# Convolution products of an attention step: one run behind the score pair instead of single products between transposes and value products

## What is computed

```
proj = h @ w_in[layer]
q, kc, vc, ksl, vsl, kwn, vwn, gts, cb, cc, ch = jnp.split(proj, split_at, axis=-1)
...
o_attn = nsa_attention(q, kc, vc, ksl, vsl, kwn, vwn, gts, rel_bias)   # compressed, selected, window branch
o_conv = short_conv(cb, cc, ch, conv_w[layer])                         # cb * conv3(cc * ch)
mixed = jnp.concatenate([rms_norm(o_attn, ...), rms_norm(o_conv, ...)], axis=-1)
x = x + mixed @ w_out[layer]
```

## Time and profile before

| | us |
|---|---|
| median of 3 executions | 2334.39 |
| lowest, highest | 2327.37, 2335.43 |
| the profiled execution | 2332.5, with a span of 2330.7 from first to last instruction |
| TensorE busy over the span | 2216.8 (95%) |
| VectorE, ScalarE, GpSimd busy | 397.0, 277.4, 70.3 |

### The profile page before, as it was taken

The page is one execution under the profiler, slowest core; times in us unless marked ns, Lnnn a source line. Parts: engine busy times, 40 slices in busy tenths (PEclk is TensorE's granted clock), DMA queues, the critical chain, the costliest instruction groups (busy, mean ns, idle before and its releaser), DMA issues.

```text
span 2330.7 us, 29764 instructions
## 1 busy us (share of the span) xinstructions
PE 2216.8 (95%) x12796; PEld 1665.9 (71%) x12796; DVE 397.0 (17%) x1080; ACT 277.4 (12%) x752; POOL 70.3 (3%) x79
## 2 busy tenths in 40 slices
PE   7999998999999989999966999999999999999994
PEld 3556644444444445566556999999999999999994
DVE  2235422000000022254231001010000101010102
ACT  1133311000000012233100000000000000000000
POOL 1100000000000011000000000000000000000001
PEclk9999998999999989999967999999999999999997
DMA  8101106222210402000018556767777777878743
GB/s 322 56 37 37 37 9 266 77 72 72 83 62 0 200 9 72 37 37 1 1 50 356 218 221 244 282 257 287 272 281 276 277 290 283 308 289 304 289 181 118
DMA packets 43987, 382.83 MB, mean 164 GB/s; under 512 B 5362, under 2 KB 5394, under 8 KB 14544
## 3 DMA queue, kind: packets, MB, share of 16 engines
q1 hardware_dynamic: 36208, 355.68, 41.0%
q0 software_dynamic: 4768, 14.92, 2.0%
q10 hardware_dynamic: 2880, 10.32, 1.1%
HBM read 368.46 MB, written 14.54 MB: 164 GB/s over the span
## 4 chain that ended last, share of the span: by engine, by line
PE 93%; DVE 3%; DMA 1%; issue 1%; ACT 1%; POOL 1%; POOLq 0%; DVEq 0%; ACTq 0%
PE ps L382 29%; PE ps L391 14%; PE ps L1022 13%; PE ps L855 7%; PE ps L1031 6%; PE ps L795 6%; PE ps L1007 5%; PE ps L920 2%; PE ps L911 2%; PE ps L898 2%; PE ps L801 1%; PE ps L868 1%; DVE work L1079 1%; PE ps L363 1%; PE ps L339 1%
## 5 line engine op out<-in xcount | busy, mean ns | idle before, releaser
L382 PE MATMUL ps<-work,arena 128*128 128x136 f32 (+3 forms) x5632 | 704.8, 284 | 0.7 <-issue 0.7
L382 PEld LDWEIGHTS ps<-work,arena 128*128 128x128 f32 x5632 | 686.9, 192 | 1.2 <-issue 0.8
L391 PE MATMUL ps<-hid,arena 128*128 128x136 f32 (+3 forms) x2816 | 364.7, 283 | 0.0
L391 PEld LDWEIGHTS ps<-hid,arena 128*128 128x128 f32 x2816 | 348.4, 191 | 0.1
L1022 PE MATMUL ps<-hT,arena 128*128 128x512 f32 x704 | 304.6, 596 | 0.8 <-issue 0.8
L1022 PEld LDWEIGHTS ps<-hT,arena 128*128 128x128 f32 x704 | 134.8, 192 | 170.1 <-issue 170.1
L552 DVE TENSOR_TENSOR hid<-sg,ps 128x136 f32<-128x136 f32 (+3 forms) x176 | 52.8, 300 | 900.2 <-ACT sg L653 899.6
L855 PE MATMUL ps<-hT,arena 128*128 128x512 f32 x384 | 197.6, 617 | 2.0 <-ACT gc L1386 2.0
L653 ACT ACTIVATE sg<-ps 128x136 f32<-128x136 f32 (+3 forms) x176 | 50.5, 287 | 928.4 <-PE ps L382 928.4
L1031 PE MATMUL ps<-arena 128*128 128x512 f32 x352 | 151.3, 593 | 0.8 <-DVE arena L1310 0.8
L795 PE MATMUL ps<-arena,hT 128*128 128x512 f32 (+1 forms) x384 | 131.9, 503 | 0.0
(11 more groups left out here) (201 smaller groups left out, 991.1 us busy)
## 6 DMA issues: line engine op xcount, KB each, us to landing
arena<-m_w SPq DMA_DIRECT2D x176, 1536.0 KB, 6.6
arena<-f_gu SPq DMA_DIRECT2D x22, 1024.0 KB, 5.0
arena<-w_cv SPq DMA_DIRECT2D x8, 1536.0 KB, 21.6
arena<-f_dn SPq DMA_DIRECT2D x11, 1024.0 KB, 4.8
arena<-w_o SPq DMA_DIRECT2D x4, 2048.0 KB, 7.5
arena<-w_q SPq DMA_DIRECT2D x2, 2048.0 KB, 12.0
arena<-w_kv SPq DMA_DIRECT2D x2, 2048.0 KB, 16.3
arena<-bias_by_query_and_key SPq DMA_DIRECT2D x2, 2048.0 KB, 8.8
```

What stands on the lines that cost most here:

```text
L382: m = mm(ps[:, s % 2, j * CAP:j * CAP + W], w[:, k, :], xT[:, k, 0:W], start=(k == 0), stop=(k == KD - 1))
L391: m = mm(ps[:, 2 + j // 2, (j % 2) * CAP:(j % 2) * CAP + W], down_w[s % NSLOT][:, j * P:(j + 1) * P], hid[:, s % 2, 0:W], start=(s == 0 an ...
```

## The change

One table is replaced. It still holds 80 products in 30 steps, and a third still ends at steps 2, 5, 8, ..., 29, as before.

```
-STEP_FILL = ((1, 1, 1), (1, 1, 1), (1, 1, 0)) + 2 * ((0, 1, 1), (1, 1, 1), (1, 1, 1)) + (
-    (0, 1, 3), (1, 1, 1), (0, 1, 0), (0, 1, 1), (1, 1, 1), (1, 1, 1), (0, 1, 1), (0, 1, 1), (0, 1, 3),
-    (0, 1, 1), (1, 1, 1), (1, 1, 1), (0, 1, 1), (1, 1, 1), (1, 1, 1), (0, 1, 1), (0, 1, 3), (1, 0, 1),
-    (0, 1, 1), (1, 1, 1), (1, 1, 1))
+STEP_FILL = 10 * ((3, 0, 0), (3, 0, 0), (2, 0, 0))
```

## The result

| | before | after |
|---|---|---|
| median | 2334.91 us (4 executions) | 2362.47 us (4 executions) |
| lowest, highest | 2327.37, 2335.86 | 2360.91, 2363.44 |
| profiled execution, span | 2332.5, 2330.7 | 2361.65, 2359.8 |
| loop of layer 0, first scores to sum of squares | 168.59 | 183.11 |
| loop of layer 1 | 165.26 | 181.44 |

The kernel after is slower by 27.6 us, a ratio of 1.0128 (95% interval 1.0114 to 1.0143). The two loops are 14.5 and 16.2 us longer, 30.7 together; the span grew by 29.1, so the rest of the program became 1.6 us shorter, 1.5 of it behind the second loop; why is open.

What follows compares the result with a forecast made beforehand. TensorE, holding 93% of the chain, was taken as the bound. Waits of 10.2 + 4.4 + 2.2 - 2.6 = 14.2 us a layer, 28.4 in both, plus about 4 for the clock, gave 2365 us, range 2349 to 2392.

Steps and rivals of the forecast that it cites:

- Term 1: In each step, VectorE's copy out of bank 2 loses its covering product between the turns: 10.2 us a layer.
- Term 2: Thirds starting directly behind the scores wait for reads of bank 3, at steps 6, 9, 15, 18: 4.4 us a layer.
- Term 3: VectorE's combine and conv_taps at step 9 delay the second turn of step 10: a wait of 2.2 us, before 0.70.
- a sign against terms 2 and 3: In the profile after, no wait longer than 1.5 us would show these two terms wrong.
- Term 4: The loop's earlier idle time other than steps 30 and 31 goes away: 2.6 us a layer saved.
- Term 5: Clock falls after longer waits in the loops: 2.5 more falls at 1.7 us, about 4 us, between 0 and 17.
- The rival of many falls: The clock falls again and again, at every start of a third: 31 us on top of 28, 2393 us; chance 0.17.
- The rival of the covered waits: VectorE and ScalarE are on time, leaving only term 1 and step 6: 18 us, 2352 us; chance 0.13.
- the one on the other side: Products ahead of the first turn buffer VectorE, so second turns find the copy made: 2327 us; chance 0.03 for faster.

Runs made afterwards that it cites:

- one_as_cover: The kernel after with one product of each run put back between the two turns, (2, 1, 0), (2, 1, 0), (1, 1, 0): 2347.6 us.
- reads_first: The kernel after, table kept, with VectorE's conv_z and ScalarE's conv_c moved earlier in their lists and VectorE's conv_taps one step later: 2363.2 us.
- double_copy_after: The kernel after with VectorE's copy out of bank 2 made twice, the second behind the first: 2405.3 us.
- run_block0: The kernel before with the runs of the kernel after only in steps 0 to 8 (block 0): 2337.1 us.
- best_tail: The kernel before with ScalarE's conv_c ahead of the compressed probabilities and three of the last third's products moved into step 30: 2322.8 us.
- best_taps: best_tail with VectorE's conv_taps one step later on top: 2321.8 us, ratio 0.9953 to the kernel before.

## Why the prediction was right, and where it wasn't

**The size.** 2365 was forecast and 2362.5 measured; over the median before it, 31 forecast and 27.6 measured. The parts: without their falls the loops are 180.5 and 180.0 us long after, 165.3 and 165.3 before (layer 0 before less the 3.3 us by which it exceeds layer 1; after, the 2.6 us of step 18 and the 1.4 of a fall at step 30 of layer 1 taken off). That is 15.2 and 14.8 us of waits against 14.2 forecast. The clock, net, cost 0.7 us against 4, the rest of the program gained 1.6. That the total came within 3 us is in part luck: the waits were 1.6 us more than forecast, the rest of the program 1.6 us less, and only the clock was left. The forecast's own sum is 2366.4 us on the median (2364.5 and 1.9), not 2365.

**Term 1 was right, block by block.** Forecast from turn to turn 0.75, 0.99, 1.23, 1.48 us; read 0.75, 0.98, 1.24, 1.47. The row of step 26 in the kernel before, which has no product between its turns, carried it. one_as_cover gives its sum, about 10 us a layer for 10.2, and the doubled copy its cause. The view lists 20 of the some 30 such waits forecast; the others are hidden behind the modelled ends.

**Term 2 was right in most of its ends and wrong in one of its waits.** Step 6: 1.34 forecast, 1.33 read (157.27 + 0.42 to 159.02). Step 18: the product was to start 5.3 us after the turn and started after 5.27. Step 9: 0.5 forecast, 0.5 read. Step 15 was mis-sized: 0.4 forecast, 0.9 and 0.6 us in the two layers. ScalarE's chain there (exponential, two copies, `conv_c`) is set off by the second turn of step 14, and from that turn to the product it is 2.5 and 2.2 us, of which TensorE fills 1.6. That the second turn itself is late adds nothing: in one_as_cover, where it isn't, the view lists the same 0.8 us at this place. What the term left out is the value product behind combine, at steps 9, 17 and 25. The kernel before covers it with the triple (0, 1, 3), so its trace has no such wait; `o_read` stands in the list of the change and could have been followed. At steps 9 and 17 the omission changed nothing: the 1.1 and 1.0 us waited there are missing from the waits at steps 10 and 18, where VectorE's list, not TensorE's, sets the end. At step 25 nothing stands behind it, and its 1.0 us came on top.

**Term 3 was right as an end** (7.8 us forecast, 7.74 read), and split over two waits as just said. The prediction had named a sign against terms 2 and 3, no wait longer than 1.5 us, and by the view it came true: besides the 1.7 us of step 30, which was there before, the longest wait is 1.27. The two waits of over 2 us at steps 10 and 18 don't exist; in each place two waits of 0.6 to 1.1 us make up that length. The sign was the wrong one for ends that are counted rightly. In time, terms 2 and 3 rest on these ends, since reads_first, which takes their waits away, gained nothing. **Term 4** was right within what the loops show.

**Term 5 was mis-sized.** Three waits of over 1 us a layer were to bring 2.5 falls more; the number of stretches stayed at two, one of them twice as long as either in the loops before. Counting waits didn't tell the falls in the experiments either: reads_first has fewer waits and more falls. The rival of many falls (2393 us) didn't come about in this kernel, but in one_as_cover and double_copy_after the clock was low for 31 and 34 us, so it was a fair one. The rival of the covered waits fails by the waits at steps 10 and 18, the one on the other side by the turns: in each of the four steps shown, the second turn waits.

## What to carry to other kernels

When one engine sets the end and hands a buffer to another, what stands between the hand-over and the next use of that buffer is worth the hand-over's latency and no more: here one product of 0.86 us between two turns saved 0.22 to 0.49 us each time. Look in the trace for the one place that already lacks this cover by chance, and measure from start to start, since waits shorter than a matmul's modelled end don't show as idle. To find where a late reader's list sets the end, count to that end and not wait by wait; and when a wait is gone, look for the products behind it that want the same reader.

## What was not expected of the hardware

In the loops the granted clock fell to its lower level (1.2 GHz) only at places where TensorE had waited 0.6 us or more among turns, value products and scores, but not at all such places, and for 3.4 or 6.8 us each time. Two traces of the kernel after have the same two stretches within 0.4 us of each other, and loops equal to 0.05 us; yet the kernel before varies by 10 us between executions, longer where the mean clock is lower. So the 3.3 us that its one trace has in layer 0 may not be there each time, and a difference of a few us between single traces can be such a fall. Nor do the falls grow with the waits: 15 us of idle time a loop went with 10 us at low clock in both loops together, and 11.8 us with 20. In three kernels there was none in either loop: in run_block0 at waits of up to 1.7 us, in best_tail and best_taps at 0.7 us and less. What decides between two places of like waits is open; no run here isolates it. For the size of a change it matters as much as a term of the sum: 3.3 us in layer 0 of the kernel before, and most of what reads_first had gained in waits.
